# Two of six groups of modulation weights moved from the first stage to behind the output products and into the routing

## The chip, the cores and the metric

The kernel runs on one core of one Trainium2 chip. The metric is the time on the device in microseconds, from the start to the end of the one launch. All data are float32.

## The reference, cut to what matters

The program is a two-part network on 256 tokens of width 1024. The first part mixes the tokens by attention and then sends each token to 4 of 32 experts. The second part is a stack of two layers that are steered by "modulation" rows; these depend on nothing but the two condition vectors `c` and `c_ctx`:

```python
# first part
mix = token_mixer(x, w_in, sinks, w_proj_a, w_proj_b, w_out, slopes)      # attention
x = layer_norm(DEEPNORM_ALPHA * x + mix, ln1_g, ln1_b)
ffn = moe_ffn(x, router_w, ..., w_gate, w_up, w_down, ...)                # top 4 of 32 experts
x = layer_norm(DEEPNORM_ALPHA * x + ffn, ln2_g, ln2_b)
# second part, for each layer i in (0, 1)
m  = (silu(c)     @ w_mod[i] + b_mod[i]).reshape(bsz, 6, d)
mc = (silu(c_ctx) @ w_mod[i] + b_mod[i]).reshape(6, d)
h_lat = x * (1.0 + s1) + sh1
h_ctx = ctx * (1.0 + s1c) + sh1c
```

`w_mod` is 2 x 1024 x 6144 float32: 48 MB, which the kernel reads as 24 chunks of 2 MB. A result of layer 0 is first used in the expert stage, where the context rows are prepared beside the experts; a result of layer 1 is used much later.

## The kernel before, in words

The kernel is a sequence of blocks. In a block each engine runs its own list of instructions, the lists are tied by semaphores, and the next block begins on every engine only when all of them have come to the end of the block. The blocks that matter are `attention`, `route` and `moe`, in this order.

**The ring.** All large weights pass through a ring of six slots of 2 MB each in SBUF (`Ring`, lines 128 to 178). `program` writes down the chunks in one fixed list; chunk n goes to slot n mod 6 until late in the expert stage. SyncE (SP) issues the transfers in the order of the list (`Ring.load`, L148); ahead of each it waits until the earlier user of the slot is done. So the transfers are one queue in one order, at most six chunks ahead of what is being used, and SP can issue nothing else while it waits.

**Order of the list before.** `w_in0`; then six times one of `w_in1` to `w_in6` followed by four modulation chunks (one group); then `w_in7` to `w_in10`, `w_proj_a` (1 MB), two `w_proj_b`, two `w_out`; then the six chunks of each expert, `moe0.0` to `moe0.5` for expert 0.

**First stage (in `attention`).** TensorE multiplies x by `w_in0` to `w_in6` (queries, keys, values). After each chunk from `w_in1` on it takes one modulation group (`modulation(i)`, L379): four small products with the bias, then for each of four chunks 8 products in which only two columns (the two condition vectors) stand in the array. ScalarE copies the four pairs of result rows out of PSUM (L552), and GpSimd (POOL) stores them to HBM with four small DMAs (L322). The part is DMA, TensorE and ScalarE by turns, with PSUM banks that are handed over by semaphores.

**Attention units.** When all of q, k and v are copied (`qkv_ready`), 24 units follow, one group of heads and one block of queries each: scores (L464), bias and maximum on VectorE, exponential on ScalarE (L596), transposes (L482), products with v (L500). Between them TensorE computes a third of a gate tile per unit from `w_in7` to `w_in10` (L442).

**End of `attention`.** TensorE forms the projections, VectorE merges them (L698, L700), and TensorE forms the output products with `w_out` in four pieces (L179). VectorE adds x and normalises (L709 to L714). Its last addition ends the block. SP meanwhile issues the expert chunks up to `moe0.3` as slots come free, waits for `merged_ready`, loads the two rows of the norm (`lns`), and issues `moe0.4` and `moe0.5`.

**`route`.** SP loads the router's weights and biases (L1143), then the ring up to `moe0.5` (nothing is left to issue before the change), then the context rows `ctx` (1 MB, L1145), and waits for `ctx_in` before it leaves the block. TensorE turns y (L1158), forms the logits of two tiles (L179), waits for `gates_known`, and forms the placing products (L179, L1180). VectorE runs a chain of small steps for each tile (top 4, softmax, one-hot sums) and then the places.

**`moe`.** SP first loads nine small or middle pieces for the context (`Context.begin`, L828 to L834) and then goes on with the ring. TensorE adds the bias of the down projection, gathers the tokens of the first experts, and takes `moe0.0`; only then is a slot free for `moe1.0`. From here to the end nothing of the order is touched by the change.

Of the kernel before, what the change touches and what calls it, by code (L numbers as in the profile page):

```python
# [24 lines left out]
KT = D // P  # L25
# [10 lines left out]
N_IN = 11  # L36
N_MOD = 2 * 6 * D // (4 * 512)
START_PARTS = 4
ALPHA1 = 2.0 ** 0.25
# [225 lines left out]

def attention(nc, d, m, M, banks, ring):

# [33 lines left out]

    c = rows[:, 3592:3608].rearrange("p (k s) -> p k s", k=KT)
    silu_c = rows[:, 3608:3624].rearrange("p (k s) -> p k s", k=KT)
    bias = m.part(15872, 512)
    stage = m.part(12800, 2, 512)
    n_mod = N_MOD
    mods = banks.plan([("mod", i) for i in range(n_mod)], [6, 7])
# [4 lines left out]
    gx = banks.plan([("x", i) for i in range(4)], [4, 5, 6, 7])  # L312

    with nc.Block() as block:

        @block.gpsimd
        def _(pool):
            for i in range(n_mod):
                pool.wait_ge(M("mod_staged"), i + 1)
                for g in range(4):  # L320
                    col = (4 * (i % (n_mod // 2)) + g) * 512
                    pool.dma_start(d["mod"][i // (n_mod // 2), :, col:col + 512], stage[32 * g:32 * g + 2, i % 2, :])\  # L322
                        .then_inc(M(f"mod_out{i % 2}"), 16)
            for i in range(2):
                pool.wait_ge(M(f"mod_out{i}"), 64 * (n_mod // 2))

        @block.sync
        def _(sp):
            first = m.ring[:, ring.slot("w_in0"), :].rearrange("p (k j) -> p k j", k=KT)
            first_src = d["w_in"][0].rearrange("p (k j) -> p k j", k=KT)  # L330
            for i in range(START_PARTS):
                ks = slice(i * KT // START_PARTS, (i + 1) * KT // START_PARTS)
                sp.dma_start(xT[:, ks, :], d["xT"][:, ks, :]).then_inc(M(f"start_in{i}"), 16)
                sp.dma_start(first[:, ks, :], first_src[:, ks, :])\
                    .then_inc(M(f"start_in{i}" if i + 1 < START_PARTS else f"chunk_in{ring.slot('w_in0')}"), 16)
            ring.sent = 1
            sp.dma_start(c, d["c"]).then_inc(M("c_in"), 16)
            sp.dma_start(bias[0:4 * n_mod, :], d["b_mod"]).then_inc(M("c_in"), 16)
# [12 lines left out]
        @block.tensor  # L351
        def _(pe):
# [26 lines left out]

            def modulation(i):  # L380
                where = mods["mod", i]
                banks.wait_free(pe, where)
                if i == 0:
                    pe.wait_ge(M("consts_in"), 16)
                    pe.wait_ge(M("c_in"), 32)
                    pe.wait_ge(M("silu_ready"), 1)
                for g in range(4):
                    nc.tensor.matmul(m.ps[32 * g:32 * g + 2, where[0], :], ident[0:4 * n_mod, 4 * i + g:4 * i + g + 1].to_broadcast([4 * n_mod, 2]),
                                     bias[0:4 * n_mod, :], start=True, stop=False, skip_group_check=True)
                for quarter in range(4):  # L390
                    name = f"w_mod{4 * i + quarter}"
                    w = ring.wait(pe, name).rearrange("p k j -> p (k j)").rearrange("p (k j) -> p k j", k=2)
                    for k in range(2):
                        for g in range(4):
                            last = nc.tensor.matmul(m.ps[32 * g:32 * g + 2, where[0], :], silu_c[:, 2 * quarter + k, :],
                                                    w[:, k, g * 512:(g + 1) * 512], start=False, stop=quarter == 3 and k == 1,
                                                    skip_group_check=True)
                    if quarter < 3:
                        ring.used(last, name)
                banks.fill(last, where)  # L400
                done_with(name, where)

            first_chunk()
            for n in range(2, 10):
# [14 lines left out]
            for i in range(4):  # L419
# [104 lines left out]
            for i in range(4):  # L524
# [6 lines left out]
                if t:  # L531
                    pe.wait_ge(M(f"bank_full{where[0]}"), where[1] + 1)
                    ring.done(pe, "w_out", half)

        @block.scalar
        def _(act):
            act.wait_ge(M("c_in"), 32)
            nc.scalar.activation(silu_c, c, ACT.Silu).then_inc(M("silu_ready"), 1)
# [4 lines left out]
            def mod_out(i):  # L543
                where = mods["mod", i]
                banks.wait_full(act, where)
                if i >= 2:

                    act.wait_ge(M(f"mod_out{i % 2}"), 64 * (i // 2))
                for g in range(4):
                    which = (4 * (i % (n_mod // 2)) + g) // 2  # L550
                    rows_ = slice(32 * g, 32 * g + 2)
                    last = nc.scalar.activation(stage[rows_, i % 2, :], m.ps[rows_, where[0], :], ACT.Copy,  # L552
                                                bias=1.0 if which in (SCALE1, SCALE2) else 0.0)
                banks.free(last, where)
                act.wait_ge(M(f"bank_free{where[0]}"), where[1] + 1)
                act.sem_inc(M("mod_staged"), 1)

            for n in range(10):
# [7 lines left out]
                if n % 2 and n > 3:  # L566
                    mod_out(n // 2 - 2)
            where = gp["kb", 0]
# [3 lines left out]
            for i in range(4):  # L572
# [48 lines left out]
            for t in range(TT):  # L621
                norm_act(nc, act, m, M, n0 + t + 1)

        @block.vector
        def _(dve):
# [56 lines left out]
            for u in range(len(units)):  # L682
# [3 lines left out]
                if u == 1:  # L686
                    for i in range(2):
                        dve.wait_ge(M(f"mod_out{i}"), 64 * (n_mod // 2))
                if u:
# [440 lines left out]

def route(nc, d, m, M, banks, ring):


    x = Experts(m)
    turn = banks.plan([("t", i) for i in range(4)], [4, 5, 6, 7])
    small = banks.plan([("logit", t) for t in range(TT)] + [("place", t) for t in range(TT)] + ["total", "gT"], [0, 1, 2, 3])
    with nc.Block() as block:

        @block.sync
# [9 lines left out]
        def _(pe):  # L1149
# [12 lines left out]
            for t in range(TT):  # L1162
# [21 lines left out]
        def _(act):  # L1184
# [2036 lines left out]
def program(nc, d, out):  # L3221
    with ExitStack() as ctx:
# [24 lines left out]
        ring = Ring(M, m.ring, chunks)  # L3247
        attention(nc, d, m, M, banks, ring)
        route(nc,d,m,M,banks,ring)
        moe(nc,d,m,M,banks,ring)  # L3250
# [96 lines left out]
```

## Time and profile before

| | us |
|---|---|
| median of 3 runs | 3646.48 |
| the runs | 3639.62, 3647.6, 3646.48 |
| the profiled execution, own time | 3643.52 |
| its span, first to last instruction | 3641.7 |
| mean granted TensorE clock, share of full | 0.97 |
| DMA, mean over the span | 379 GB/s |

Times in rows count from the start of the span. PE is TensorE, PEld its weight load, DVE VectorE, ACT ScalarE, POOL GpSimd; SPq is SyncE's instruction that issues a DMA. In a timeline row stand the start, the length, the engine, the line of the kernel, the operation, out<-in, the count of merged instructions, and in brackets the idle time before them and what ended it. Lines such as L148 or L179 are those of helpers, so the tile's name tells the use. A float32 product is recorded as two instructions. Of the granted clock 1.00 is 2.4 GHz and 0.50 is 1.2 GHz.

### The profile page before, as it was taken

The numbers are of one execution on the slowest core, as the hardware profiler recorded it, in microseconds if no ns is written. First come the engines' busy times: TensorE is split into PE (matmuls) and PEld (weight loads), VectorE is DVE, ScalarE is ACT, GpSimd is POOL, SyncE is SP. The second block draws the span as 40 slices with busy tenths as digits, with TensorE's granted clock in tenths as the row PEclk, the third lists the DMA queues.
The fourth block names the chain that finished last, engine by engine and source line by source line (L and its number), as shares of the span: only waits on it lengthen the run. The fifth ranks groups of instructions, "written<-read, shape, count | busy, mean of one in ns | idle before, by whom it ended". The sixth has DMA issues, their size and how long they took to land. (4 is left out here: it accounts for less than half of the span.)

```text
span 3641.7 us, 34378 instructions
## 1 busy us (share of the span) xinstructions
PE 3219.5 (88%) x11268; PEld 1436.6 (39%) x11268; DVE 1761.2 (48%) x4096; ACT 1088.3 (30%) x2958; POOL 862.0 (24%) x796
## 2 busy tenths in 40 slices
PE   8898899999999996988888878998888978788776
PEld 6476443344334432433344323333334444222222
DVE  0053211111130124776775677668764466766665
ACT  1131111111111112344343344445334123433433
POOL 0100000000000002443444444444441014444432
PEclk9999899999999998999999999999999989999999
DMA  9934799999999999999999999999997149999997
GB/s 406 427 118 152 289 408 416 422 417 425 412 428 428 399 428 374 408 421 422 421 417 409 420 420 415 407 417 415 419 413 303 49 191 421 421 421 420 417 411 328
DMA packets 158245, 1379.94 MB, mean 379 GB/s; under 512 B 18601, under 2 KB 19113, under 8 KB 26610
## 3 DMA queue, kind: packets, MB, share of 16 engines
q0 software_dynamic: 111360, 805.46, 53.5%
q1 hardware_dynamic: 46706, 572.24, 37.7%
q8 instruction: 94, 1.54, 0.2%
q14 instruction: 85, 0.70, 0.0%
HBM read 1376.48 MB, written 1.15 MB: 378 GB/s over the span
## 5 line engine op out<-in xcount | busy, mean ns | idle before, releaser
L2701 PE MATMUL ps<-sb_arena,sb_diag 128*128 128x512 f32 x3072 | 1498.4, 626 | 337.3 <-ACT sb_diag L2678 335.4
L2604 POOL DMA_INDIRECT sb_arena<-in_uv,sb_idx x768 | 849.3, 1106 | 2586.2 <-POOLq L1278 1229.0
L2637 DVE SCALAR_TENSOR_TENSOR sb_arena<-sb_arena,sb_H 128x1024 f32<-128x1024 f32 x768 | 940.8, 1226 | 623.5 <-DMA sb_arena<-in_uv,sb_idx 418.6
L2701 PEld LDWEIGHTS ps<-sb_arena,sb_diag 128*128 128x128 f32 x3072 | 565.3, 196 | 1226.4 <-ACT sb_diag L2678 657.1
L1357 PE MATMUL ps<-sb_ring,sb_arena 128*64 128x512 f32 x3072 | 674.3, 594 | 3.6 <-DMA sb_ring<-in_moe 3.6
L2669 ACT ACTIVATE sb_act<-sb_dots 128x1 f32<-128x1 f32 x768 | 155.0, 202 | 1102.7 <-DVE sb_arena L2637 1100.9
L1357 PEld LDWEIGHTS ps<-sb_ring,sb_arena 128*64 128x64 f32 x3072 | 214.4, 137 | 441.5 <-issue 430.5
L2678 ACT ACTIVATE sb_diag<-sb_consts,sb_act 128x128 f32<-128x128 f32 x768 | 308.4, 402 | 26.7 <-PE ps L2701 1.6
L1547 DVE TENSOR_SCALAR sb_arena<-ps 128x512 f32<-128x512 f32 x32 | 22.1, 692 | 591.4 <-PE ps L1357 575.7
L2673 ACT ACTIVATE sb_act<-sb_act,sb_wts 128x1 f32<-128x1 f32 x768 | 226.2, 295 | 24.9
L179 PE MATMUL ps<-sb_ring,sb_arena 128*128 128x512 f32 x416 | 182.0, 594 | 1.9 <-DVE sb_arena L700 1.3
L179 PEld LDWEIGHTS ps<-sb_ring,sb_arena 128*128 128x128 f32 x416 | 77.8, 190 | 97.4 <-issue 95.6
L645 DVE SCALAR_TENSOR_TENSOR sb_H<-sb_X,ps 128x128 f32<-128x128 f32 (+1 forms) x56 | 17.8, 346 | 182.8 <-PE ps L464 182.7
L1554 DVE TENSOR_SCALAR sb_arena<-ps 128x512 f32<-128x512 f32 x32 | 22.1, 692 | 155.1 <-PE ps L1357 155.1
L1461 ACT ACTIVATE sb_arena<-sb_arena 128x512 f32<-128x512 f32 x32 | 20.2, 630 | 249.6 <-DVE sb_arena L1547 249.6
L179 PE MATMUL ps<-sb_arena,sb_ring 128*128 128x256 f32 (+1 forms) x480 | 92.0, 352 | 1.9 <-ACT sb_arena L3055 0.8
L1455 ACT ACTIVATE sb_arena<-ps 128x512 f32<-128x512 f32 x32 | 19.1, 597 | 246.2 <-PE ps L1334 246.2
L1478 ACT ACTIVATE sb_arena<-ps 128x512 f32<-128x512 f32 x32 | 19.1, 597 | 227.5 <-PE ps L1357 227.5
L2034 PE MATMUL ps<-sb_ring 128*128 128x512 f32 x192 | 86.3, 592 | 0.0
L179 PEld LDWEIGHTS ps<-sb_arena,sb_ring 128*128 128x128 f32 x480 | 81.0, 190 | 11.8 <-issue 1.8
L1348 PE MATMUL ps<-sb_arena 64*128 64x512 f32 x264 | 67.1, 628 | 9.4 <-issue 9.4
L179 PE MATMUL ps<-sb_ring 128*128 128x256 f32 (+2 forms) x320 | 72.5, 381 | 1.4 <-ACTq L3049 1.0
(347 smaller groups left out, 2374.6 us busy)
## 6 DMA issues: line engine op xcount, KB each, us to landing
sb_ring<-in_moe SPq DMA_DIRECT2D x192, 2048.0 KB, 16.3
sb_ring<-in_w_mod SPq DMA_DIRECT2D x24, 2048.0 KB, 20.3
sb_ring<-in_w_in SPq DMA_DIRECT2D x10, 2048.0 KB, 25.6
sb_ring<-in_a_w_in SPq DMA_DIRECT2D x8, 2048.0 KB, 13.4
sb_ring<-in_b_w_in SPq DMA_DIRECT2D x8, 2048.0 KB, 11.9
sb_ring<-in_w_q SPq DMA_DIRECT2D x6, 2048.0 KB, 11.4
sb_arena<-in_uv,sb_idx POOLq DMA_INDIRECT x768, 15.2
sb_ring<-in_a_w_out SPq DMA_DIRECT2D x4, 2048.0 KB, 16.3
```

The source lines that it names most:

```text
L179: last = nc.tensor.matmul(out, lhs, rhs, start=i == 0, stop=i == len(pairs) - 1)
L1348: last = nc.tensor.matmul(acc[2 * t + n], x.weighT[rows, t * P:(t + 1) * P], x.ye[rows, :], start=False, stop=ends, skip_group_check=True)
L1357: last = nc.tensor.matmul(m.ps[n * SLOTS:(n + 1) * SLOTS, bank, :], lhs(k + KT // 2 * (c % 2), n), w[:, k, n * 512:(n + 1) * 512], start=f ...
L1547: nc.vector.tensor_scalar(x.g, m.ps[:, 4, :], LIMIT, None, ALU.min).then_inc(M(name("g_ready", p)), 1)
L1554: nc.vector.tensor_scalar(x.u, m.ps[:, 5, :], LIMIT, -LIMIT, ALU.min, ALU.max).then_inc(M(name("u_ready", p)), 1)
L2034: last = nc.tensor.matmul(m.ps[:, where[0], :], lhs(k), w[:, k, :], start=k == 0, stop=k == KT - 1)
L2604: pool.indirect_dma_start(uv[n_ % BUFS], None, table, bass.IndirectOffsetOnAxis(m.idx[:, pair % 2, k:k + 1], 0))\
L2637: nc.vector.scalar_tensor_tensor(out=u, in0=u, scalar=1.0, in1=m.H[:, order[i], :], op0=ALU.mult, op1=ALU.mult, accum_out=m.dots[:, n_ % P ...
L2669: nc.scalar.activation(a, m.dots[:, n_ % PK:n_ % PK + 1], ACT.Gelu_apprx_tanh).then_inc(M("gelu_done"), 1)
L2673: nc.scalar.activation(a, a, ACT.Copy, scale=m.wts[:, pair % 2, k:k + 1]).then_inc(M("act_ready"), 1)
L2678: nc.scalar.activation(m.diag[n_ % DIAGS], m.const("ident"), ACT.Copy, scale=a).then_inc(M("diag_ready"), 1)
L2701: last = nc.tensor.matmul(out[h], m.diag[n_ % DIAGS], uv[b][:, D + h * 512:D + (h + 1) * 512], start=opens, stop=ends)
```

## The change

`LATE_MODS = 2`. The chunks of modulation groups 4 and 5 (`w_mod16` to `w_mod23`) leave their places behind `w_in5` and `w_in6` and stand in the list behind `w_out`, ahead of `moe0.0`. The code of a group moves into a class `Modulation` with one function for each engine. Group 4 is computed at the end of `attention`, behind the output products; group 5 in `route`, between the logits and the wait for `gates_known`. In `attention` SP now issues the ring up to `w_mod16`, waits for `merged_ready`, loads the norm's rows, and issues `w_mod17` to `w_mod23`; the six chunks of expert 0 are all left to `route`, where `ring.load` stands ahead of `ctx`. `route` gets a GpSimd part, which stores group 5 and waits until all stores have landed. The condition vectors move from `H` to `wts`, since `H` takes the norm's rows before group 4 is computed.

```diff
@@
+LATE_MODS = 2
@@
+class Modulation:
...
+    def tensor(self, pe, i):
+        nc, m, M, banks, ring, where = self.nc, self.m, self.M, self.banks, self.ring, self.where[i]
+        banks.wait_free(pe, where)
...
+        for g in range(4):
+            nc.tensor.matmul(m.ps[32 * g:32 * g + 2, where[0], :],
+                             m.const("ident")[0:4 * N_MOD, 4 * i + g:4 * i + g + 1].to_broadcast([4 * N_MOD, 2]),
+                             self.bias[0:4 * N_MOD, :], start=True, stop=False, skip_group_check=True)
+        for quarter in range(4):
+            name = f"w_mod{4 * i + quarter}"
+            w = ring.wait(pe, name).rearrange("p k j -> p (k j)").rearrange("p (k j) -> p k j", k=2)
+            for k in range(2):
+                for g in range(4):
+                    last = nc.tensor.matmul(m.ps[32 * g:32 * g + 2, where[0], :], self.silu_c[:, 2 * quarter + k, :],
+                                            w[:, k, g * 512:(g + 1) * 512], start=False, stop=quarter == 3 and k == 1,
+                                            skip_group_check=True)
+            if quarter < 3:
+                ring.used(last, name)
+        banks.fill(last, where)
+        pe.wait_ge(M(f"bank_full{where[0]}"), where[1] + 1)
+        ring.done(pe, name)
+
+    def scalar(self, act, i):
...
+        banks.wait_full(act, where)
+        if i >= 2:
+
+            act.wait_ge(M(f"mod_out{i % 2}"), 64 * (i // 2))
+        for g in range(4):
...
+            last = nc.scalar.activation(self.stage[rows_, i % 2, :], m.ps[rows_, where[0], :], ACT.Copy,
+                                        bias=1.0 if which in (SCALE1, SCALE2) else 0.0)
+        banks.free(last, where)
+        act.wait_ge(M(f"bank_free{where[0]}"), where[1] + 1)
+        act.sem_inc(M("mod_staged"), 1)
+
+    def store(self, pool, i):
+        pool.wait_ge(self.M("mod_staged"), i + 1)
+        for g in range(4):
+            col = (4 * (i % (N_MOD // 2)) + g) * 512
+            pool.dma_start(self.d["mod"][i // (N_MOD // 2), :, col:col + 512], self.stage[32 * g:32 * g + 2, i % 2, :])\
+                .then_inc(self.M(f"mod_out{i % 2}"), 16)
@@ attention, gpsimd
-            for i in range(n_mod):
...
+            for i in range(early):
+                mod.store(pool, i)
             for i in range(2):
-                pool.wait_ge(M(f"mod_out{i}"), 64 * (n_mod // 2))
+                pool.wait_ge(M(f"mod_out{i}"), 64 * (early // 2))
+            mod.store(pool, early)
@@ attention, sync
-            ring.load(sp, ring.at["moe0.0"] + 4)
+            ring.load(sp, ring.at["w_out"] + 3)
 
             sp.wait_ge(M("merged_ready"), KT)
             load_rows(sp, M, m, [d["lns"][i:i + 1, :] for i in range(2)], norm_rows)
-            ring.load(sp, ring.at["moe0.0"] + PER_EXPERT)
+            ring.load(sp, ring.at["moe0.0"])
@@ attention, tensor
                     done_with(name, where)
-                    modulation(n // 2 - 1)
+                    if n // 2 <= early:
+                        mod.tensor(pe, n // 2 - 1)
@@
                     done_with(f"w_in{5 + piece}", where)
-                    modulation(4 + piece)
+                    if 4 + piece < early:
+                        mod.tensor(pe, 4 + piece)
@@
                     pe.wait_ge(M(f"bank_full{where[0]}"), where[1] + 1)
                     ring.done(pe, "w_out", half)
+            mod.tensor(pe, early)
@@ attention, scalar
-                if t:
-                    mod_out(3 + piece)
-            mod_out(5)
+                if t and 3 + piece < early:
+                    mod.scalar(act, 3 + piece)
@@
             for t in range(TT):
                 norm_act(nc, act, m, M, n0 + t + 1)
+            mod.scalar(act, early)
@@ route
+    mod.plan([N_MOD - 1], [7])
     with nc.Block() as block:
+
+        @block.gpsimd
+        def _(pool):
+            mod.store(pool, N_MOD - 1)
+            for i in range(2):
+                pool.wait_ge(M(f"mod_out{i}"), 64 * (N_MOD // 2))
@@ route, tensor
                 banks.fill(products(nc, m.ps[:, where[0], 0:NE], pairs), where)
+            mod.tensor(pe, N_MOD - 1)
             pe.wait_ge(M("gates_known"), TT)
@@ route, scalar
                 nc.scalar.activation(x.exp[:, 0:TOPK], x.exp[:, 0:TOPK], ACT.Exp).then_inc(M("top_exp"), 1)
+            mod.scalar(act, N_MOD - 1)
@@ program
-            if 1 <= n <= N_MOD:
+            if 1 <= n <= N_MOD - LATE_MODS:
                 front += [(f"w_mod{u}", d["w_mod"][u], SLOT) for u in range(4 * n - 4, 4 * n)]
         front += [("w_proj_a", d["w_proj_a"], 2 * D)]
         front += [("w_proj_b", d["w_proj_b"][n], SLOT) for n in range(2)]
         front += [("w_out", d["w_out"][n], SLOT) for n in range(2)]
+        front += [(f"w_mod{u}", d["w_mod"][u], SLOT) for u in range(4 * (N_MOD - LATE_MODS), 4 * N_MOD)]
```

## Rows read from the trace of the kernel before

**Rows 1.** Page: DMA busy share in 40 slices of 91 us each, in tenths.
```profile
DMA  9934799999999999999999999999997149999997
```

**Rows 2.** Page, DMA issues: engine, op, count, KB each, median us to landing.
```profile
sb_ring<-in_w_out SPq DMA_DIRECT2D x2, 2048.0 KB, 7.6
```

**Rows 3.** Timeline of TensorE, end of the first stage and the first unit.
```profile
123.56 3.72 PE L179 MATMUL ps<-sb_H,sb_ring 128*128 128x256 f32 x16 [2.28 <-DMA sb_ring<-in_w_in]
...
137.75 1.04 PE L388 MATMUL ps<-sb_arena,sb_consts 24*2 24x512 f32 x8
...
148.06 14.00 PE L179 MATMUL ps<-sb_ring,sb_H 128*128 128x512 f32 x32 [2.29 <-DMA sb_ring<-in_w_in]
...
170.40 1.23 PE L464 MATMUL ps<-sb_arena 64*128 64x128 f32 x12 [0.18 <-PE ps L395]
175.70 0.90 PE L482 MATMUL ps<-sb_consts,sb_H 128*128 128x128 f32 x3 [4.07 <-DVE sb_H L665]
```

**Rows 4.** Timeline of ScalarE, same stretch: last value copy, group 5's copies.
```profile
162.09 0.60 ACT L577 ACTIVATE sb_arena<-ps 128x512 f32<-128x512 f32 x1 [6.27 <-PE ps L179]
...
170.29 2.39 ACT L552 ACTIVATE sb_arena<-ps 2x512 f32<-2x512 f32 x4 [5.03 <-PE ps L395]
```

**Rows 5.** Windows: busy by engine, PEclk, DMA share, GB/s.
```profile
176.00:182.00 6.00, 6.00 (x18) 4.25 (x17) 2.11 (x7) 1.20 (x3) 0.00 (x0) 0.50 1.01 426
...
183.00:184.00 1.00, 1.00 (x6) 0.52 (x4) 0.28 (x1) 0.00 (x0) 0.00 (x0) 0.61 1.02 434
...
358.00:359.00 1.00, 0.00 (x0) 0.00 (x0) 0.86 (x2) 0.00 (x1) 0.00 (x0) 0.50 0.72 311
...
395.00:396.00 1.00, 0.86 (x6) 0.67 (x5) 0.00 (x0) 0.10 (x1) 0.00 (x0) 0.80 1.03 422
```

**Rows 6.** Timeline of TensorE, output products to the placing products.
```profile
347.98 7.11 PE L179 MATMUL ps<-sb_ring,sb_arena 128*128 128x512 f32 x16 [0.30 <-PE ps L179]
362.33 3.65 PE L1158 MATMUL ps<-sb_consts,sb_X 128*128 128x128 f32 x16 [7.25 <-PEq L314]
366.82 3.62 PE L179 MATMUL ps<-sb_arena 128*128 128x32 f32 x16 [0.84 <-DMA sb_arena<-in_b_down]
...
370.93 3.62 PE L179 MATMUL ps<-sb_arena 128*128 128x32 f32 x16
...
381.93 1.79 PE L179 MATMUL ps<-sb_arena,sb_consts 128*128 128x32 f32 x10 [6.81 <-DVEq L1225]
```

**Rows 7.** Timeline of VectorE: norm's first and last instruction of the block.
```profile
346.35 1.41 DVE L709 SCALAR_TENSOR_TENSOR sb_X<-sb_X,ps 128x512 f32<-128x512 f32 x2 [19.60 <-DMA sb_H<-in_lns]
...
360.41 1.22 DVE L714 TENSOR_TENSOR sb_X<-sb_X,sb_H 128x1024 f32<-128x1024 f32 x1
```

**Rows 8.** GpSimd's stores of a group, and their us from issue to landing.
```profile
173.01 2.04 POOL L322 DMA_DIRECT2D mod_rows<-sb_arena  x4 [5.37 <-ACTq L556]
...
DMA to landing us min/median/max: 5.4/6.6/7.9
```

**Rows 9.** Timeline of SyncE's issues, merged products to the expert stage.
```profile
325.74 1.28 SPq L148 DMA_DIRECT2D sb_ring<-in_moe  x3
327.06 1.22 SPq L755 DMA_DIRECT2D sb_H<-in_lns  x2
347.80 7.74 SPq L148 DMA_DIRECT2D sb_ring<-in_moe  x2
...
363.68 0.42 SPq L1143 DMA_DIRECT2D sb_arena<-in_b_down  x1
364.14 0.43 SPq L1145 DMA_DIRECT2D sb_X<-in_ctx  x1
385.27 0.83 SPq L828 DMA_DIRECT2D sb_H<-mod_rows  x2
...
404.04 34.09 SPq L148 DMA_DIRECT2D sb_ring<-in_moe  x9
```

**Rows 10.** Windows, VectorE's chain in the routing (columns as in group 5).
```profile
370.00:375.00 5.00, 5.00 (x23) 4.79 (x22) 3.19 (x15) 0.20 (x1) 0.00 (x0) 0.50 0.00 0
```

More of the change, by code:

```diff
@@ L261, in distances, with __init__, plan @@
     return out
-def attention(nc, d, m, M, banks, ring):
+class Modulation:
+    def __init__(self, nc, d, m, M, banks, ring):
+        self.nc, self.d, self.m, self.M, self.banks, self.ring = nc, d, m, M, banks, ring
+        self.c = m.wts[:, 0, 0:2 * KT].rearrange("p (k s) -> p k s", k=KT)
+        self.silu_c = m.wts[:, 0, 2 * KT:4 * KT].rearrange("p (k s) -> p k s", k=KT)
+        self.bias = m.part(15872, 512)
+        self.stage = m.part(12800, 2, 512)
+        self.where = {}
+    def plan(self, groups, places):
+        self.where.update(self.banks.plan(groups, places))
+    def tensor(self, pe, i):
+        nc, m, M, banks, ring, where = self.nc, self.m, self.M, self.banks, self.ring, self.where[i]
+        banks.wait_free(pe, where)
+        if i == 0:
+            pe.wait_ge(M("consts_in"), 16)
+            pe.wait_ge(M("c_in"), 32)
+            pe.wait_ge(M("silu_ready"), 1)
+        for g in range(4):
[16 more added lines that the diff above has]
+    def scalar(self, act, i):
+        nc, m, M, banks, where = self.nc, self.m, self.M, self.banks, self.where[i]
+        banks.wait_full(act, where)
+        if i >= 2:
+            act.wait_ge(M(f"mod_out{i % 2}"), 64 * (i // 2))
+        for g in range(4):
+            which = (4 * (i % (N_MOD // 2)) + g) // 2
+            rows_ = slice(32 * g, 32 * g + 2)
+            last = nc.scalar.activation(self.stage[rows_, i % 2, :], m.ps[rows_, where[0], :], ACT.Copy,
[9 more added lines that the diff above has]
+                .then_inc(self.M(f"mod_out{i % 2}"), 16)
@@ L269, in attention @@
+def attention(nc, d, m, M, banks, ring, mod):
     qk = m.part(0, 21, T)
@@ L296, in attention @@
     gp = banks.plan(proj, [0, 1, 2, 3])
[L302 to L307, printed above, removed]
+    early = N_MOD - LATE_MODS
+    mod.plan(range(early), [6, 7])
     go = banks.plan([("o", u) for u in range(len(units))], [6])
@@ L312, in attention @@
     gx = banks.plan([("x", i) for i in range(4)], [4, 5, 6, 7])
+    mod.plan([early], [0])
     with nc.Block() as block:
@@ L317, in _ @@
         def _(pool):
-            for i in range(n_mod):
[L319 to L323, printed above, removed]
+            for i in range(early):
+                mod.store(pool, i)
             for i in range(2):
-                pool.wait_ge(M(f"mod_out{i}"), 64 * (n_mod // 2))
+                pool.wait_ge(M(f"mod_out{i}"), 64 * (early // 2))
+            mod.store(pool, early)
         @block.sync
@@ L336, in _ @@
             ring.sent = 1
-            sp.dma_start(c, d["c"]).then_inc(M("c_in"), 16)
-            sp.dma_start(bias[0:4 * n_mod, :], d["b_mod"]).then_inc(M("c_in"), 16)
+            sp.dma_start(mod.c, d["c"]).then_inc(M("c_in"), 16)
+            sp.dma_start(mod.bias[0:4 * N_MOD, :], d["b_mod"]).then_inc(M("c_in"), 16)
             ring.load(sp, 2)
@@ L378, in done_with @@
                 ring.done(pe, name)
[L380 to L401, printed above, removed]
             first_chunk()
@@ L537, in _ @@
             act.wait_ge(M("c_in"), 32)
-            nc.scalar.activation(silu_c, c, ACT.Silu).then_inc(M("silu_ready"), 1)
+            nc.scalar.activation(mod.silu_c, mod.c, ACT.Silu).then_inc(M("silu_ready"), 1)
             def pair_of(n):
                 return gates[:, 2 * n:2 * n + 2, :].rearrange("p a b -> p (a b)")
[L543 to L556, printed above, removed]
             for n in range(10):
@@ L566, in _ @@
                 if n % 2 and n > 3:
-                    mod_out(n // 2 - 2)
+                    mod.scalar(act, n // 2 - 2)
             where = gp["kb", 0]
@@ L687, in _ @@
                     for i in range(2):
-                        dve.wait_ge(M(f"mod_out{i}"), 64 * (n_mod // 2))
+                        dve.wait_ge(M(f"mod_out{i}"), 64 * (early // 2))
                 if u:
@@ L1128, in __init__, with route @@
         self.select = m.part(3072, SLOTS)
-def route(nc, d, m, M, banks, ring):
+def route(nc, d, m, M, banks, ring, mod):
     x = Experts(m)
@@ L3247, in program @@
         ring = Ring(M, m.ring, chunks)
-        attention(nc, d, m, M, banks, ring)
-        route(nc,d,m,M,banks,ring)
+        mod = Modulation(nc, d, m, M, banks, ring)
+        attention(nc, d, m, M, banks, ring, mod)
+        route(nc, d, m, M, banks, ring, mod)
         moe(nc,d,m,M,banks,ring)
```

## The prediction

> **What bounds the kernel now.** I read the slices of the page first: the DMA engines are nearly full in almost every slice, and the reader is to see the hole in slices 3 to 5, some 180 to 450 us [rows 1]. The change takes 16 MB from ahead of this hole and puts it into it. What that is worth is decided by the hole alone, so next I read the timelines of TensorE, ScalarE and SyncE at its two edges and the issues at its end [rows 3, 4, 6, 9]. They show three stretches with three limits.
>
> First stage: TensorE gets `w_in5` at 123.56 and `w_in6` at 148.06, each after a wait on its transfer [rows 3]. Five chunks lie between: 24.5 / 5 = 4.90 us a chunk. The stage goes at the pace of the DMA, with TensorE close behind it (2.29 us of slack in 24.5).
>
> Attention units and projections: the ring is full and the transfers rest; the engines set the pace.
>
> End of `attention` and `route`: the last VectorE step ends at 361.63 [rows 7], TensorE is in the next block at 362.33 [rows 6]. The routing then hangs on small steps; the DMA engines do nothing for whole windows [rows 10], and SyncE is in `moe` at 385.27. The first chunk after the six that were already there is requested at 404.04, 18.8 us later, when `moe0.0` has been used [rows 9].
>
> Everything behind the start of `moe` begins relative to it, with the same six chunks in the ring. So the change is worth the shift of that one point. I keep all times on the clock of the kernel before and add the shift of the first stage at the end.
>
> **Part 1: the first stage, 18.4 us gained.** `w_in5` keeps its place in the list, so it still lands at 123.56. `w_in6` now follows directly and lands 4.9 later, at 128.5. But TensorE is not ready for it: the products with `w_in5` last until 137.75 [rows 3]. Then it needs 14.00 for those with `w_in6`: 151.75. Before, the copy of the last values hid behind group 5's products; now the scores wait for it: 0.63 from end to end (162.06 to 162.69) [rows 3, 4], and about 0.1 for the signal. Scores start at 152.5 instead of 170.40: 17.9 gained. Eight chunks are 39.2 us of transfers, but less than half of that shows, because TensorE becomes the limit. By another way: two groups of products (137.75 to 145.77, 8.0; 162.1 to 170.2, 8.1) and the wait of 2.29 go, 0.6 comes: 17.8.
>
> In the first unit ScalarE is no longer busy with group 5's copies until 172.68 [rows 4], so the wait of 4.07 before the first transposes [rows 3] shrinks. It can't all go, since VectorE has the bias and maximum of two units to do in it. Below 0 and above 4.07 are excluded; I take 0.5. Together 18.4. The clock is half at 176 to 183 and rises in the window 183 to 184 [rows 5]; if TensorE no longer loses it there, up to 4 us more come. I take that it does, since most of the wait stays.
>
> The gate weights `w_in7` to `w_in10` now land by 148, and the chunks of the projections have the same slots' users ahead of them as before. Nothing waits for them. VectorE's wait for the stores in the second unit falls on stores long landed: 0. SyncE prefetches one chunk during the units, `w_mod16` in place of `moe0.0`.
>
> **Part 2: group 4 behind the output products, 6.5 us lost.** After `merged_ready` SyncE issues the norm's rows and then `w_mod17` to `w_mod19`, in place of three expert chunks and then the rows [rows 9]. Before, the last of this landed at 346.35, when VectorE got the rows [rows 7]; the same 7 MB now end at the same time. The rows come earlier, but VectorE's second tile waits for TensorE, whose products end at 355.09 [rows 6]: worth 0. TensorE needs the four chunks of group 4 at 355.2: no wait. The group takes 8.0 as it did from 137.75 to 145.77: 363.3, and most of it hides beside the norm, which ends at 361.63. The copies do not hide: 2.39 on ScalarE [rows 4]: 365.7. Then GpSimd, 0.33 later, issues four stores in 2.04 [rows 8]: 368.1. This is the block's last work, 6.5 behind the old end. TensorE starts `route` at 368.8, SyncE at 368.6. GpSimd doesn't wait for the landing here. Bounds: 1.7 (copies and stores free of charge), and 8.5 (stores slower by half).
>
> SyncE requests `w_mod20` when `w_out`'s first half is free (347.8), `w_mod21` at 355.2 [rows 9], `w_mod22` and `w_mod23` when the first and second chunk of group 4 are used, at 355.2 + 1.0 + 1.75 = 358.0 and at 359.8. A chunk that finds the queue empty lands 7.6 after its request [rows 2]. So they land at 355.4, 362.8, 367.7 and 372.6.
>
> **Part 3: the routing, another 21.8 us lost.** The router's weights are requested 6.5 later than before and stand behind `w_mod23`: before, the logits waited for them until 366.82, 3.1 after the request [rows 6, 9]; now they land at about 374.2. The logits run from 374.2 to 382.5 (8.3, as 366.82 to 375.18 before, at half clock [rows 6, 10]). `moe0.0` and `moe0.1`, requested right behind the router's pieces, land by 379 and 384.
>
> Now group 5. Its chunks are there. At full clock it takes 8.0, at half clock 16. The clock is half when it starts, since it fell within 4 us of TensorE's stop at 355 [rows 5] and will fall in the wait after group 4 too. It came back 10 us after `moe`'s products began at 385.3 [rows 5, 9], and 8 us after those at 175.7 [rows 3, 5]; the 8.3 us of logits before did not bring it back [rows 10]. I take half clock for the first two quarters: `w_mod20` is used at 382.6 + 2.1 + 3.5 = 388.2, `w_mod21` at 391.7, the group ends at about 395.4 (bounds 390.7 and 398.7). VectorE's chain is done at 381.93 + 7.4 = 389.3, so the placing products now wait for the group; with their 3.3 us of tail (381.93 to 385.27 [rows 6, 9]) they would end the block at 398.7.
>
> But SyncE ends it. `moe0.2` needs the slot of `w_mod20`. It is requested at 388.2, while the queue ran dry at 384; `moe0.3` to `moe0.5` follow as slots come free, none later than the queue can take them. Behind them stands `ctx`, 1 MB, and SyncE waits for it. The sum: 388.3 + 2.7 (7.6 - 4.9, until the first chunk moves) + 4 x 4.9 + 2.5 = 413.1. Before, `ctx` was requested at 364.14 with nothing ahead of it and was long there. GpSimd's stores: ScalarE's copies end at 397.8, the stores are issued by 400.2, and land within 5.4 to 7.9 [rows 8], at 408: under the cover of `ctx`. If that cover goes, they hold the block at 408.
>
> Of these stores the Trainium skill says ("DMA: Bandwidth & Descriptors", Queues, rings and completion order) that each DMA engine goes round robin between the queues that have work, packet by packet. By that rule they don't stand behind the five chunks of SyncE's queue, and the landing of 6.6 taken beside a full queue agrees [rows 8]; if they stood in one line with the chunks, they would land at about 413 and change the sum by nothing.
>
> `moe` thus starts at 413.1 + 0.5 = 413.6 in place of 385.27: 28.3 later, of which 6.5 are part 2 and 21.8 part 3. The tensor clock is half at both starts and the first request of `moe` stays 18.8 behind: no difference. Part 1 gives 18.4 back. **Sum: +9.9 us, in round numbers +10.**
>
> **The rivals.**
>
> *The queue stays dense.* If the clock is back when group 5 starts, `w_mod20` is used at 382.6 + 2.8 = 385.4, `ctx` lands at 410.3, and the sum is +7.1. If the clock is full for the logits too, the queue never runs dry: 384 + 19.6 + 2.5 = 406.1, and the sum is +3 (the stores hold it no longer than this). For it: TensorE is at work without a break from 374.2. Against it: the half clock of the logits [rows 10]. The Trainium skill ("TensorE: Matmul & The Clock Gate", Part 1) has it that sustained busy time brings the clock back, whatever is multiplied. By that rule group 5 would find the full clock after the 8.3 us of logits. The 10 us in `moe` leave it open.
>
> *The boundary is not held by the queue (the other side).* This takes a `ctx` that lands ahead of the expert chunks, or stores and `ctx` both early. Then TensorE's chain ends the block at 398.7: +13.4 - 18.4 = -5.0, and with full clock in group 5 at 394.0: -9.7. It decides from the point at which `ctx` and the stores land by 403.2. For it: a lone `ctx` needs no more than a lone chunk. Against it: the norm's rows, 1 MB behind three chunks, landed only with the last of them, 19 us after the request [rows 7, 9].
>
> *The first stage gives more or less.* The clock is kept in the first units (22.4 in place of 18.4: sum +6), or the first unit gains nothing and part 2 costs 8.5 (+12.5), and a gap opens between `moe0.2` and `moe0.3` when both are late (+15).
>
> **How the numbers follow.** The forecast has 0.60, the dense queue 0.15, the unheld boundary 0.10, the kept clock 0.10, the dearer ones 0.05. The profiled execution took 3643.52, of which 3641.7 is the span: 3643.52 + 10.0 = 3653.5. Its median of runs is 3 above, the mean of all four times 0.8 above, so I say 3654. From no change the measurement can tell about 0.2%, which is 7.3 us: of the forecast's share some 0.50 is above that, the dearer ones add 0.05, the others 0.05: slower 0.60; faster is the end of the unheld boundary and what I haven't seen, 0.08; the rest is 0.32. The likeliest case alone spans +5 to +15, that is 3649 to 3659. Down to the kept clock with a dense queue (-1) and up to +16: 3643 to 3661.
>
> **What would show it.** Right: scores start at about 152.5; `attention` ends on GpSimd's stores; group 5 runs at half clock at its start; SyncE's wait for `ctx` ends `route` on the changed kernel's own clock near 395; `moe` starts about 10 us later than 385.27 and the rest is shifted. Wrong: an end of `route` on VectorE or TensorE, a `ctx` that lands before `moe0.5`, scores not before 155, or a rest of the kernel whose length differs from before by more than 3 us.

## The result and the profile after

| us | before | after |
|---|---|---|
| median of 5 runs | 3640.2 | 3663.04 |
| lowest to highest | 3639.16 to 3647.6 | 3659.74 to 3664.46 |
| the profiled execution, own time | 3643.52 | 3663.16 |
| its span | 3641.7 | 3661.3 |

The ratio of the runs is 1.0049, with a 95% interval of 1.0037 to 1.0062: the change makes the kernel slower by 0.49%, about 18 us (13 to 23 by the interval). The two medians are further apart, 22.8 us, since the five runs before lie in two groups, near 3640 and near 3647; the differences below go by the ratio. The two profiled executions are 19.6 us apart. I had forecast slower, by 10 us; the sign and the place are right, the size is not, and the median lies 2 us above the range.

The page's slices show that the hole in the DMA engines' work is not filled: it begins a slice earlier, and slices 2 to 5 have 6, 2, 5 and 7 tenths where [rows 1] has 9, 3, 4 and 7.
```profile
DMA  9625799999999999999999999999997149999997
```
Everything behind the first request of `moe` is untouched. In the windows of the two kernels from there to the end of the expert stage (columns as in [rows 5]), 986.0 and 985.9 us do the same work:
```profile
404.00:1390.00 986.00, 978.95 (x4761) 400.68 (x4756) 174.99 (x401) 127.89 (x213) 0.00 (x0) 1.00 0.98 415
```
```profile
423.87:1409.80 985.93, 978.90 (x4760) 400.60 (x4756) 174.98 (x401) 128.00 (x213) 0.00 (x0) 1.00 0.98 415
```
So the account closes at that request: 404.04 before [rows 9], 423.87 after, 19.8 us later. SyncE's issues in the kernel after:
```profile
308.57 32.57 SPq L149 DMA_DIRECT2D sb_ring<-in_w_mod  x7
356.06 0.33 SPq L1172 DMA_DIRECT2D sb_arena<-in_router_w  x1
...
358.07 22.22 SPq L149 DMA_DIRECT2D sb_ring<-in_moe  x6
380.33 0.45 SPq L1174 DMA_DIRECT2D sb_X<-in_ctx  x1
399.73 0.81 SPq L850 DMA_DIRECT2D sb_H<-mod_rows  x2
...
423.87 10.63 SPq L149 DMA_DIRECT2D sb_ring<-in_moe  x4
```
Its TensorE, which answers to [rows 3, 6]:
```profile
138.28 13.97 PE L180 MATMUL ps<-sb_ring,sb_H 128*128 128x512 f32 x32 [0.30 <-PE ps L180]
152.98 1.26 PE L500 MATMUL ps<-sb_arena 64*128 64x128 f32 x12 [0.73 <-ACTq L600]
157.83 0.90 PE L518 MATMUL ps<-sb_consts,sb_H 128*128 128x128 f32 x3 [3.58 <-DVE sb_H L687]
...
328.92 7.10 PE L180 MATMUL ps<-sb_ring,sb_arena 128*128 128x512 f32 x16 [0.30 <-PE ps L180]
...
337.14 7.05 PE L297 MATMUL ps<-sb_ring,sb_wts 128*2 128x512 f32 x64
356.26 3.65 PE L1187 MATMUL ps<-sb_consts,sb_X 128*128 128x128 f32 x16 [12.07 <-PEq L374]
360.68 3.60 PE L180 MATMUL ps<-sb_arena 128*128 128x32 f32 x16 [0.78 <-DMA sb_arena<-in_b_down]
...
368.88 1.88 PE L289 MATMUL ps<-sb_arena,sb_consts 24*2 24x512 f32 x8
370.69 9.11 PE L297 MATMUL ps<-sb_ring,sb_wts 128*2 128x512 f32 x64
...
399.75 7.16 PE L1347 MATMUL ps<-sb_arena 32*128 32x512 f32 x8 [18.25 <-PEq L1160]
```
GpSimd's two late groups of stores, answering to [rows 8]:
```profile
347.24 2.05 POOL L325 DMA_DIRECT2D mod_rows<-sb_arena  x4 [203.79 <-ACTq L319]
382.61 2.05 POOL L325 DMA_DIRECT2D mod_rows<-sb_arena  x4 [33.31 <-DVEq L1160]
```
The landing of the first of these groups, and then that of `ctx` (min, median and max us from the issue):
```profile
DMA to landing us min/median/max: 5.5/5.6/6.2
...
DMA to landing us min/median/max: 19.0/19.0/19.0
```
The stretches, each as the difference of its length in the two kernels:

| stretch | before | after | difference |
|---|---|---|---|
| start to out products' end | 355.09 | 336.02 | -19.1 |
| from there to SyncE's first request in `route` | 7.04 | 20.04 | +13.0 |
| `route`, to SyncE's first request in `moe` | 23.14 | 43.67 | +20.5 |
| from there to the first chunk request | 18.77 | 24.14 | +5.4 |
| sum | | | +19.8 |

The reader is to see two waits that end a block. The first block has its last instruction, the stores' issue, at 349.29, and the next one begins at 356.06, when the stores issued up to 349.3 have been in flight for their 5.5 to 6.2. The second has nothing to do on any engine from 384.66 on; `ctx`, requested at 380.33, lands at 399.3, and 0.4 later `moe` begins.

### The profile page after: what moved, and what is told of

Same layout as the page of the kernel before. It is cut to its first block and busy times, and to the rows that moved or that the text cites. A ratio compares the mean times of both kernels' runs of the same rounds, so it can differ in the third digit from the quotient of the medians.

```text
span 3661.3 us, 34379 instructions
## 1 busy us (share of the span) xinstructions
PE 3215.5 (88%) x11268; PEld 1430.4 (39%) x11268; DVE 1762.2 (48%) x4096; ACT 1088.4 (30%) x2958; POOL 862.4 (24%) x796
## 3 DMA queue, kind: packets, MB, share of 16 engines
HBM read 1376.48 MB, written 1.15 MB: 376 GB/s over the span
## 5 line engine op out<-in xcount | busy, mean ns | idle before, releaser
L325 POOL DMA_DIRECT2D mod_rows<-sb_arena x24 | 12.5, 528 | 371.7 <-ACTq L319 338.4
L1486 ACT ACTIVATE sb_arena<-ps 128x512 f32<-128x512 f32 x32 | 19.1, 597 | 258.4 <-PE ps L1365 258.4
L1509 ACT ACTIVATE sb_arena<-ps 128x512 f32<-128x512 f32 x32 | 19.1, 597 | 227.5 <-PE ps L1388 227.5
## 6 DMA issues: line engine op xcount, KB each, us to landing
sb_ring<-in_w_in SPq DMA_DIRECT2D x10, 2048.0 KB, 24.2
```

## The experiments

The verdicts rest on three numbers: the start of `moe` (SyncE's, or TensorE's where SyncE waits for stores first), the first chunk request in it, and the ratio to the kernel before, measured beside it. All but e9 build on the changed kernel. Each difference below is against it, unless the kernel before is named. The intervals of e1, e2, e4 and e5 overlap that of the change (1.0037 to 1.0062), so for these four the rows show what moved, and the times only agree with it.

**e1, the stores of group 4 later.**
```diff
 # attention, gpsimd
-            mod.store(pool, early)
 # route, gpsimd
+            mod.store(pool, N_MOD - 2)
             mod.store(pool, N_MOD - 1)
```


> Edit: the four stores of group 4 leave attention and are issued by GpSimd in the routing, just ahead of those of group 5. Theory A (the block attention ends only when GpSimd's stores have landed, which I had priced at their issue alone): SyncE's first router request moves from 356.1 to about 347.2, 0.5 behind ScalarE's copies, which end at 346.6; the router's pieces then stand behind w_mod23 and the logits start at about 355.5 in place of 360.7; the rest follows, so moe starts 5 us earlier and the kernel is 5 us faster than the changed one. Rival (the block's end hangs on something else, such as SyncE's requests or TensorE): first router request stays at 356, time unchanged.

Measured: 3655.7 us, ratio 1.0036 (1.0023 to 1.0048). SyncE of e1, and the logits on its TensorE:
```profile
346.84 0.33 SPq L1172 DMA_DIRECT2D sb_arena<-in_router_w  x1
...
397.24 0.81 SPq L849 DMA_DIRECT2D sb_H<-mod_rows  x2
...
417.99 19.19 SPq L149 DMA_DIRECT2D sb_ring<-in_moe  x5
```
```profile
358.27 3.62 PE L180 MATMUL ps<-sb_arena 128*128 128x32 f32 x16 [8.02 <-DMA sb_arena<-in_b_down]
```
The block ends 9.2 earlier, right behind ScalarE's copies: theory A holds. But most of the gain is used up at once: the logits now wait 8.02 for the router's pieces behind `w_mod23` and start only 2.4 earlier, and so does `moe` (2.5). I had said 5. The first request comes 5.9 earlier, because the stretch from the start of `moe` is shorter too, 20.8; what that stretch is worth is taken up further down.

**e2, `ctx` ahead of the expert chunks.**
```diff
+            sp.dma_start(m.X[:, 2:4, :], d["ctx"]...).then_inc(M("ctx_in"), 16)
             ring.load(sp, ring.at["moe0.0"] + PER_EXPERT)
-            sp.dma_start(m.X[:, 2:4, :], d["ctx"]...).then_inc(M("ctx_in"), 16)
```


> Edit: in the routing the context rows are requested ahead of the six expert chunks. Theory B (the routing ends when ctx lands behind the expert chunks): ctx lands before 365, and the block ends when group 5's stores have landed, at about 391 in place of 399.7; 8 to 9 us faster than the changed kernel. Rival (the expert chunks themselves are what the next stage waits for, so that an earlier start gives nothing): moe starts at 391 but the first request of moe stays at 423.9, time unchanged.

Measured: 3656.49 us, ratio 1.0033 (1.0022 to 1.0043). GpSimd and SyncE of e2:
```profile
383.91 2.05 POOL L325 DMA_DIRECT2D mod_rows<-sb_arena  x4 [33.44 <-DVEq L1160]
```
```profile
357.51 0.33 SPq L1172 DMA_DIRECT2D sb_arena<-in_router_w  x1
...
394.00 0.81 SPq L850 DMA_DIRECT2D sb_H<-mod_rows  x2
...
418.18 19.18 SPq L149 DMA_DIRECT2D sb_ring<-in_moe  x5
```
`route` takes 36.5 in place of 43.7, and ends 8.0 behind the issue of the last stores: theory B holds, and the next wait, which GpSimd's part of `route` has in its program, is where I put it. `moe` starts 5.7 earlier where I had said 8 to 9. The rival falls, since the first request moves with the start, by 5.7.

**e3, both.**


> Edit: both of the above. Theory A and B together: moe starts at about 386, 14 us earlier than in the changed kernel, and the time is 14 us lower, about 5 us over the kernel before. Rival (the queue of chunks sets the start in any case): no more than the gain of the better of the two alone, 8 us.

Measured: 3649.85 us, ratio 1.0018 (1.0009 to 1.0028). SyncE of e3:
```profile
391.56 0.81 SPq L849 DMA_DIRECT2D sb_H<-mod_rows  x2
...
412.37 27.22 SPq L149 DMA_DIRECT2D sb_ring<-in_moe  x7
```
The two add up: `moe` starts 8.2 earlier (2.5 and 5.7) and the first request comes 11.5 earlier (5.9 and 5.7). That is less than the 14 expected, since the logits still wait for the router's pieces as in e1. A good half of the loss is explained by two waits for data that the next block does not need at once.

**e4, TensorE kept busy until `moe`.**
```diff
             banks.fill(last, where)          # transposes of the gates, end of route
+            for _ in range(20):
+                nc.tensor.matmul(m.ps[:, 6, :], ident, m.consts[:, 0:512], start=True, stop=True)
```


> Edit: 20 products of 128x512 behind the transposes of the gates in the routing, into a bank nobody reads, so that TensorE is busy in the 18 us in which it waited for the block's end. Nothing else is changed. Theory C (5.4 of the 19.8 us lost lie in the half clock that lasts until 422.7, 23 us into moe, where before it lasted 10): moe starts at 399.7 as in the changed kernel, its first request comes 13 to 14 us later in place of 24.1, and the time is about 10 us lower. Rival (the first request waits for a transfer or for VectorE, the clock is hidden): first request stays 24 us behind the start, time unchanged. If the added products outlast the wait because they run at half clock, moe starts later and the gain is smaller.

Measured: 3654.49 us, ratio 1.0037 (1.0023 to 1.0052). TensorE and SyncE of e4:
```profile
381.90 17.33 PE L1213 MATMUL ps<-sb_consts 128*128 128x512 f32 x40
400.38 4.89 PE L1349 MATMUL ps<-sb_arena 32*128 32x512 f32 x8 [1.15 <-PEq L1160]
```
```profile
400.35 0.81 SPq L850 DMA_DIRECT2D sb_H<-mod_rows  x2
...
417.16 22.62 SPq L149 DMA_DIRECT2D sb_ring<-in_moe  x6
```
The first request comes 16.8 behind the start in place of 24.1. That is the way of theory C, but not a proof of it: two executions of one kernel differ by 5.8 in this stretch (e7 and e10, below). By the ratio the gain is some 4 us where I had said 10. What the trace does show is the clock: it was full when `moe` began, fell to half 2 to 3 us into it although TensorE was busy, and came back at 409.5.

**e5, group 5 alone.**
```diff
-LATE_MODS = 2
+LATE_MODS = 1
 # attention: group 4 stays behind w_in5; nothing of it behind the output products
```


> Edit: LATE_MODS = 1. Group 4 stays in the first stage, group 5 alone goes into the routing; SyncE's order as in the changed kernel. Theory (the routing costs more than the first stage gives, for each group by itself): the first stage gives 8 (one group's 8.1 of products; the wait of 2.3 for w_in6 stays, 0.6 for the bare copy comes, 0.5 in the first unit), attention ends 0 later, the routing is 20 longer as in the changed kernel because ctx stands behind four chunks that wait for group 5, and moe's first request comes 24 in place of 19 behind its start: +12 with the clock as before, +17 with the clock of the changed kernel, against the kernel before. Rival (the loss of the changed kernel comes from group 4 at the end of attention and what it delays): no slower than before, -8 to 0.

Measured: 3657.99 us, ratio 1.0034 (1.0021 to 1.0046). TensorE and SyncE of e5:
```profile
163.47 1.26 PE L498 MATMUL ps<-sb_arena 64*128 64x128 f32 x12 [0.73 <-ACTq L597]
```
```profile
355.02 0.33 SPq L1168 DMA_DIRECT2D sb_arena<-in_router_w  x1
...
398.78 0.81 SPq L846 DMA_DIRECT2D sb_H<-mod_rows  x2
...
422.98 10.63 SPq L149 DMA_DIRECT2D sb_ring<-in_moe  x4
```
7 us are won at the start, `route` takes 43.8, and the first request comes 24.2 behind the start. By the ratio this is a loss of 12 us, some two thirds of that of the change, with half of what it moves; the profiled execution, 3663.31, is the slowest of the six, so its rows make the loss look larger. The rival, that the loss lies in group 4's place, falls. The group in `route` brings most of the cost there, since it holds the slots of `moe0.2` to `moe0.5`. Whether group 4 adds a loss of its own, the two overlapping intervals don't tell.

**e6, the router's rows and `ctx` requested early** (on e1).
```diff
 # attention, sync
             load_rows(sp, M, m, [d["lns"][i:i + 1, :] for i in range(2)], norm_rows)
+            for dst, src in (router, router_b, b_gate, b_up): sp.dma_start(...)   # router_in
+            sp.dma_start(m.X[:, 2:4, :], d["ctx"]...).then_inc(M("ctx_in"), 16)
 # route, sync: b_down alone is left ahead of ring.load
```


> Edit: the stores of group 4 in the routing as in e1, and the router's weights, its two biases and ctx requested by SyncE right behind the norm's rows, ahead of w_mod17; b_down alone stays in the routing. Theory (with ctx and the stores of group 4 out of the way, what is left of the loss in the routing is the wait of the logits for the router's pieces behind w_mod23, and the landing of group 5's stores): logits start at about 351.5 in place of 359 in e3, group 5 ends near 371, the stores have landed and moe starts at about 384 in place of 391.6, its first request comes 20 to 24 later, at 404 to 408, against 404.0 in the kernel before: the time is level with the kernel before, 0 to +4. Rival (the six expert chunks can't come sooner, so moe only waits for them instead): moe starts at 384, but the first request stays at 412 as in e3, +7.

Measured: 3643.15 us, ratio 0.9996 (0.9987 to 1.0006). TensorE and SyncE of e6:
```profile
351.81 3.59 PE L180 MATMUL ps<-sb_arena 128*128 128x32 f32 x16 [0.78 <-issue]
```
```profile
384.04 0.81 SPq L854 DMA_DIRECT2D sb_H<-mod_rows  x2
...
408.22 30.65 SPq L149 DMA_DIRECT2D sb_ring<-in_moe  x8
```
As forecast: level with the kernel before, with both groups moved. The rival falls, since the first request has left the 412 of e3 with the start. (The profiled execution, 3647.82, is the slowest of the ten; that its first request is 4.2 behind that of the kernel before does not contradict the ratio.)

**e7, the stores on ScalarE's queue** (on e6).
```diff
 # attention and route, scalar
             mod.scalar(act, i)
+            mod.store(act, i, "late_rows_out")
 # route: no gpsimd part
 # moe, sync
+            sp.wait_ge(M("late_rows_out"), 128)
             context.begin(sp)
```


> Edit: e6, and the stores of both late groups are issued by ScalarE behind its copies, on a semaphore of their own; SyncE waits for their landing at the start of moe, ahead of the context's pieces, and the routing has no GpSimd part. Theory (it is GpSimd's queue whose landing a block's end waits for, and the landing of group 5's stores is the last thing the routing waits for): the routing ends when ScalarE has issued the stores, at 376 to 378, first request at 396 to 402, 2 to 8 us faster than the kernel before. Rival (a block's end waits for the landing of any store): moe starts at 384 as in e6, no gain over it.

Measured: 3637.89 us, ratio 0.9985 (0.9975 to 0.9994). ScalarE, TensorE and SyncE of e7:
```profile
348.14 1.38 ACTq L325 DMA_DIRECT2D mod_rows<-sb_arena  x4
...
376.63 1.15 ACTq L325 DMA_DIRECT2D mod_rows<-sb_arena  x4
```
```profile
378.34 5.86 PE L1346 MATMUL ps<-sb_arena 32*128 32x512 f32 x8 [2.58 <-PEq L1165]
```
```profile
350.04 0.33 SPq L1169 DMA_DIRECT2D sb_arena<-in_b_down  x1
...
384.57 0.81 SPq L855 DMA_DIRECT2D sb_H<-mod_rows  x2
...
401.24 37.52 SPq L149 DMA_DIRECT2D sb_ring<-in_moe  x10
```
`moe` starts on TensorE 0.6 behind the issue of the stores; SyncE, which waits there for their landing, goes on 6.8 behind the issue, at 384.57. In `route` that alone does not compare the two queues, since in e6 GpSimd's part has a wait for the landing in its program. The end of `attention` does compare them, because no instruction waits for group 4's stores there in either kernel: with ScalarE's stores the next block begins 0.5 behind the last issue (349.52 to 350.04), with GpSimd's 6.8 behind it (349.29 to 356.06, the changed kernel). With e1 this shows that a block's end waited for the landing of GpSimd's stores and not for that of ScalarE's. The kernel now beats the one before.

**e8, e9, e10: the best, and two controls.**
```diff
 # e8 = e7 with, behind the transposes of the gates
+            for _ in range(4):
+                nc.tensor.matmul(m.ps[:, 6, :], ident, m.consts[:, 0:512], start=True, stop=True)
 # e9 = the kernel before with e6's early requests alone
 # e10 = e7
```


> Edit: e7, and 4 products of 128x512 behind the transposes of the gates, so that TensorE has no gap of 2.6 us ahead of moe. Theory (e7 still pays the half clock in the first 22 us of moe, as the changed kernel did; work without a gap ahead of moe shortens that, as in e4): moe starts 1 us later than in e7, its first request comes 14 to 17 us behind the start in place of 22.9, 4 to 7 us faster than e7. Rival (the clock falls in any case at the start of moe, since the products there are narrow): first request 20 to 23 behind the start, no gain, or 1 us lost.

> Edit, in the kernel before: only the router's weights, its two biases and ctx are requested behind the norm's rows, ahead of moe0.4; nothing of the modulation is moved. Theory (the gain of e7 is that of the moved groups once the routing is cleared for them, not of the earlier rows): the kernel before hardly waits for these rows (0.84 for the logits), so 0 to 2 us faster than before. Rival (e7 owes its gain to the earlier rows): 5 us or more faster than before.

> The kernel of e7 once more, unchanged, with five rounds, beside the two above. Theory: 4 to 7 us faster than the kernel before, as in its first measurement (ratio 0.9985). Rival (the first measurement was chance): an interval that takes in 1.

Measured: e8 3633.07 us, ratio 0.9969 (0.9958 to 0.9981); e9 3644.52 us, 1.0006 (0.9996 to 1.0015); e10 3636.64 us, 0.9981 (0.9972 to 0.9990). TensorE and SyncE of e8, SyncE of e9, and TensorE and SyncE of e10:
```profile
375.71 3.60 PE L1210 MATMUL ps<-sb_consts 128*128 128x512 f32 x8
379.61 3.68 PE L1348 MATMUL ps<-sb_arena 32*128 32x512 f32 x8 [0.30 <-PEq L1165]
```
```profile
395.02 37.52 SPq L149 DMA_DIRECT2D sb_ring<-in_moe  x10
```
```profile
384.74 0.81 SPq L833 DMA_DIRECT2D sb_H<-mod_rows  x2
...
405.56 34.09 SPq L148 DMA_DIRECT2D sb_ring<-in_moe  x9
```
```profile
377.60 5.60 PE L1346 MATMUL ps<-sb_arena 32*128 32x512 f32 x8 [2.58 <-PEq L1165]
```
```profile
394.73 37.52 SPq L149 DMA_DIRECT2D sb_ring<-in_moe  x10
```
e8 is the best of all: 0.31% below the kernel before, some 11 us. e9 gains nothing, so the early rows pay only together with the moved groups. e10 repeats e7's gain. What e8 has over e10 is in the times: its seven lie within 2.5 us (3631.78 to 3634.27), e10's eleven within 9.1 (3631.81 to 3640.95), and ten of those eleven lie above all seven. The medians are 3.6 apart, a little less than the 4 to 7 forecast. The profiles don't show where it comes from: `moe` starts 2.0 later in e8, its first request comes 15.4 behind in place of 17.1, and both end up at the same point, since the profiled execution of e10 is one of the fast ones.

## Why the prediction was right, and where its size was off

*The place, right but for 18.8 us.* The prediction let everything behind the start of `moe` be shifted. The account closes a little later, at the first chunk request there, since the stretch between the two did not stay as it was (below). From that request on the rest is shifted: 985.7 us from the first chunk request to the next stage's first issue, 985.9 before.

*Part 1, right.* Scores start at 152.98 (152.5 forecast), the wait in the first unit is 3.58 (4.07 less 0.5), and up to there 17.9 are won. The whole stage gives 19.1 (18.4). The last 1.2 come right behind that wait, where TensorE worked at half clock for 5.4 us (157.83 to 163.26) in place of 8.1 before (175.70 to 183.78 [rows 3, 5]). The window of the kernel after in which the clock rises:
```profile
163.00:164.00 1.00, 1.00 (x6) 0.66 (x5) 0.00 (x0) 0.00 (x0) 0.00 (x0) 0.87 0.00 0
```

*Part 2, mis-sized: 6.5 forecast, 13.0 measured.* The products hid beside the norm (they end at 344.2), and ScalarE and GpSimd did what was said at the time that was said: the stores are issued by 349.3, and 368.1 less 18.4 is 349.7. The failed step is the sentence "GpSimd doesn't wait for the landing here". No instruction of the kernel waits; the end of the block does. e1 takes the stores away and the block ends 9.2 earlier; e7 has them on another queue and it doesn't wait. The 6.5 are the length of the stretch, not what they cost: without the stores `moe` starts only 2.5 earlier (e1), because behind this wait stands the one for the router's pieces.

*Part 3, right: 21.8 forecast, 20.5 measured.* `ctx` behind the chunks ends the block, 0.4 after its landing; e2 shows it by taking it away. Group 5 began at half clock and got it back half way, 10.9 from 368.88 to 379.80 where I had 12.9. The dense queue did not come: when `moe0.2` is requested the queue has nothing left. Both are in one window, the clock at 0.56 on its way up and the DMA engines at nothing:
```profile
374.00:375.00 1.00, 1.00 (x12) 0.24 (x8) 0.89 (x4) 0.00 (x0) 0.00 (x0) 0.56 0.00 0
```
GpSimd's stores of group 5, issued at 382.61 while the chunks and `ctx` were still coming, landed in 5.3 to 7.3 us, so they did not stand in one line with them and were under the cover of `ctx`, as forecast.

*The start of `moe`, missed: 0 forecast, 5.4 measured.* The failed step is "The tensor clock is half at both starts and the first request of `moe` stays 18.8 behind: no difference". It is half at both starts, but it came back after 10 us before, and after 23 us here. The window of the kernel after in which it rises:
```profile
422.00:423.00 1.00, 1.00 (x6) 0.38 (x4) 0.00 (x0) 0.00 (x0) 0.00 (x0) 0.66 0.00 0
```
Sum of the misses: -0.7 + 6.5 - 1.3 + 5.4 = 9.9, which is the whole gap between +9.9 and +19.8 in the profiles.

How much of the last 5.4 belongs to the change stays open. From the start of `moe` to the first request the profiles have 18.8 (before), 20.8 (e9), 24.1 (after), 24.2 (e2, e5, e6), 20.8 (e1, e3), 22.9 (e7) and 17.1 (e10), and with products added ahead of `moe` 16.8 (e4) and 15.4 (e8). e7 and e10 are one kernel: so the same program differs by 5.8 from one execution to another, more than the 5.4 in question. The other three stretches sum to 14.4 us in the profiles, and the interval of the ratio is 13 to 23 us for the whole; as an estimate, this leaves anything from nothing to 8 us for the last. That the clock sets this stretch is shown: the longer it is half there, the longer the stretch, from 3.4 and 15.4 us in e8 to 23 and 24.2 in e2. That the change keeps it half for longer is not shown.

*The rivals.* The dense queue did not come. The clock of the first units was not kept, but it came back sooner, for 1.2 of the 4 us. The unheld boundary was the one that mattered, as a thing to build: with `ctx`, the router's rows and the stores out of the way (e7) ScalarE's issue of the stores ends `route`, 1.2 us behind VectorE's last step, and the sum turns negative, -6 in the medians, where the prediction's rival had -5.0. That the two are so close is in part luck: `moe` starts 6.9 earlier than in the kernel before, and the late clock takes some of it back.

## What to carry to other kernels

A queue in one order that crosses a barrier is a barrier for everything behind it: before weights are put into a gap, look at what small, urgent transfers stand behind them, and ask for those first. Work moved to the end of a block brings its stores along, and their landing can be what ends the block. One wait taken away can uncover the next: e1 won 9.2 us at the end of a block and 2.5 at the start of the block after it. An idle stretch on TensorE costs again after it is over, at half clock; a few products nobody reads can be cheaper than the gap (e8 against e10).

## What the runs showed of the hardware

Stores that GpSimd issued held the end of a block until they had landed, 5.5 to 6.2 us after their issue, though no instruction waits for them (after, e1); with the same stores from ScalarE's queue the next block began 0.5 us behind the issue (e7).

The granted clock does not follow TensorE's busy time in the simple way that I had expected. At the start of `moe` TensorE is busy but for two gaps of 0.7 us. The clock stood at 1.2 GHz there until 10 us behind the start (before), 15 to 16 us (e1, e3, e9) or 23 us (after, e2, e5, e6). In e7 and e10 it was still full at the start, fell 1 to 2 us into it, and came back 22 us behind the start in the one and 8 us in the other. In e4 it fell 2 to 3 us into `moe`, after 17.33 us of dense products and a gap of 1.15. The Trainium skill ("TensorE: Matmul & The Clock Gate", Part 1) has that sustained busy time brings the clock back, and warns that the point of change varies from run to run. The second half agrees in kind with e7 and e10; the first does not cover 23 us at half clock with a busy engine. The products there are 32 rows high or 128 columns wide; whether that is why, no run here shows.
